# Head sums of the recurrence in two rounded passes over high and low parts

## What is computed

```python
kk = (k * k_k).reshape(B, T, 16, 64)
kk = kk / jnp.maximum(jnp.linalg.norm(kk, axis=-1, keepdims=True), 1e-12)
k = k * (1.0 + (aa - 1.0) * k_a)
# per step of the scan, for each head
sa = S @ (-kk_t)
S = S * w_t + outer(sa, kk_t * a_t) + outer(v_t, k_t)
o_t = S @ r_t
# after it
o = (o - mu) * lax.rsqrt(var + GN_EPS)      # mean and variance over a head
bonus = jnp.sum(r * k * r_k, axis=-1, keepdims=True) * v
o = (o * ln_x_w + ln_x_b + bonus) * g
```

## Time and profile before

| | |
|---|---|
| median of 3 runs | 3679.46 us |
| lowest, highest | 3678.01, 3684.09 us |
| profiled execution, its own time | 3674.07 us |
| its span | 3672.3 us |
| mean granted TensorE clock | 0.991 |
| busy: PE, PEld, DVE, ACT, POOL | 98%, 80%, 49%, 36%, 9% |

### The profile page before, as it was taken

The page is one execution under the profiler, slowest core; times in us unless marked ns, Lnnn a source line. Parts: engine busy times, 40 slices in busy tenths (PEclk is TensorE's granted clock), DMA queues, the critical chain, the costliest instruction groups (busy, mean ns, idle before and its releaser), DMA issues.

```text
span 3672.3 us, 51366 instructions
## 1 busy us (share of the span) xinstructions
PE 3617.2 (98%) x22108; PEld 2955.7 (80%) x22108; DVE 1786.2 (49%) x2455; ACT 1310.1 (36%) x2020; POOL 327.7 (9%) x328
## 2 busy tenths in 40 slices
PE   9999999999999999999999999998999999999998
PEld 8888888877788887888888888886777777688887
DVE  5435434455543455443344354344657767555444
ACT  5544222344432232332235442224342332433222
POOL 2011101100110111110110111012000000000001
PEclk9999999999999999999999999999999999899999
DMA  6212332321323233332332123323222222532322
GB/s 228 75 55 90 97 98 92 98 70 55 100 89 106 90 98 89 95 98 92 101 95 70 55 92 95 98 92 100 83 62 78 77 63 65 178 103 89 103 91 73
DMA packets 334087, 337.56 MB, mean 92 GB/s; under 512 B 12082, under 2 KB 324004, under 8 KB 333605
## 3 DMA queue, kind: packets, MB, share of 16 engines
q1 hardware_dynamic: 333572, 334.20, 29.5%
q10 hardware_dynamic: 288, 0.09, 0.0%
HBM read 319.55 MB, written 14.68 MB: 91 GB/s over the span
## 4 chain that ended last, share of the span: by engine, by line
PE 93%; DVE 4%; ACT 2%; issue 0%; ACTq 0%; POOL 0%; POOLq 0%; DVEq 0%
PE P L99 92%; PE P L102 2%; ACT sA L114 1%; DVE lo L117 1%; DVE rw_S L117 0%; DVE aL L125 0%; DVE ds L125 0%; DVE x L125 0%; DVE x L117 0%; ACTq L160 0%; POOL acc L117 0%; DVE sA L125 0%; DVE rw_k L125 0%; DVE rw_S L125 0%; ACT hi L113 0%
## 5 line engine op out<-in xcount | busy, mean ns | idle before, releaser
L99 PE MATMUL P<-aH,lo 128*128 128x512 f32 x2840 | 1132.4, 399 | 14.4 <-DVE aL L125 7.1
L99 PE MATMUL P<-aH,hi 128*128 128x512 f32 x2840 | 1109.8, 391 | 0.0
L99 PE MATMUL P<-aL,hi 128*128 128x512 f32 x2840 | 1109.5, 391 | 0.0
L113 ACT ACTIVATE hi<-raw 128x1024 fp32r<-128x1024 f32 (+2 forms) x617 | 611.5, 992 | 1026.1 <-PE P L99 1021.6
L117 DVE TENSOR_TENSOR lo<-raw,hi 128x1024 fp32r<-128x1024 f32 (+2 forms) x617 | 742.0, 1219 | 239.1 <-ACT hi L113 239.0
L99 PEld LDWEIGHTS P<-aH,lo 128*128 128x128 f32 x2840 | 534.9, 188 | 143.1 <-issue 21.4
L99 PEld LDWEIGHTS P<-aH,hi 128*128 128x128 f32 x2840 | 534.5, 188 | 112.9
L99 PEld LDWEIGHTS P<-aL,hi 128*128 128x128 f32 x2840 | 535.4, 189 | 109.4 <-issue 3.4
L99 PE MATMUL P<-bH,lo 128*128 128x512 f32 x1088 | 423.9, 390 | 0.6 <-DVE hold L117 0.6
L99 PE MATMUL P<-bL,hi 128*128 128x512 f32 x1088 | 423.7, 389 | 0.0
L99 PE MATMUL P<-bH,hi 128*128 128x512 f32 x1088 | 423.7, 389 | 0.0
(11 more groups left out here) (289 smaller groups left out, 3834.4 us busy)
## 6 DMA issues: line engine op xcount, KB each, us to landing
raw<-in_w_ffn_in_dram SPq DMA_DIRECT2D x176, 512.0 KB, 3.6
raw<-in_w_in_dram SPq DMA_DIRECT2D x163, 512.0 KB, 3.8
raw<-in_w_ffn_out_dram SPq DMA_DIRECT2D x96, 384.0 KB, 3.0
raw<-in_w_ffn_dram SPq DMA_DIRECT2D x36, 512.0 KB, 3.8
raw<-in_w_o_dram SPq DMA_DIRECT2D x26, 512.0 KB, 3.4
raw<-in_w_ffn_dram SPq DMA_DIRECT2D x32, 384.0 KB, 3.3
raw<-in_w_mem_kv_dram SPq DMA_DIRECT2D x16, 512.0 KB, 6.1
raw<-in_w_ffn_out_dram SPq DMA_DIRECT2D x16, 512.0 KB, 3.4
```

What stands on the lines that cost most here:

```text
L99: return self.e.matmul(out, l, r, start=start, stop=stop, skip_group_check=skip) if self.e else Nothing()
L113: return self.e.activation(out, in_, func, scale=scale)
```

## The change

Two of the three head sums, of the keys' squares and of the bonus, no longer use one F32 matmul. Their operand is split like the others: ScalarE copies it in rounded form (`parts[:, 0]`), VectorE writes the rest (`parts[:, 1]`), and TensorE adds two F32R matmuls with the same block of ones, which is exact in the rounded form (`bR`, written in place of `K_BONES` once at the start). The third sum, of the variance, reads the same bits of `bR` as F32 in one full matmul. The tile `parts` lies over memory that is idle at this time, so no buffer is added. Two new steps, `rw_unit_low` and `rw_bonus_low`, hold VectorE's subtractions, and the guessed costs are set anew, so `arrange` lays out the list again. No DMA is changed.

```diff
-    out += [vec("rw_lora", pe=2.6, dve=1.75, wait=1.9), vec("rw_unit", dve=0.5, gap=0.8, gives=[("kk2", p)])]
+    out += [vec("rw_lora", pe=2.6, dve=1.75, wait=1.9), vec("rw_unit", dve=0.5, gap=1.5, gives=[("kk2 high", p)])]
     out += proj("v", 2, 2)
-    out += [Step("rw_square", p, u, pe=0.9, needs=[("kk2", p)]), vec("rw_norm", dve=0.68, gap=2.6, gives=[("inverse", p)])]
+    out += [vec("rw_unit_low", dve=0.69, wait=0.0, needs=[("kk2 high", p)], gives=[("kk2", p)])]
+    out += [Step("rw_square", p, u, pe=0.5, needs=[("kk2", p)]), vec("rw_norm", dve=0.68, gap=2.6, gives=[("inverse", p)])]
...
-            vec("rw_bonus", dve=1.45, needs=[("shift", "r", p), ("key", p)], gives=[("rk", p)]), vec("rw_centre", dve=1.4),
-            vec("rw_decay", pe=0.9, dve=1.4, hold=True, needs=[("rk", p)]), vec("rw_turn", 0, pe=0.6),
+            vec("rw_bonus", dve=1.45, needs=[("shift", "r", p), ("key", p)], gives=[("rk high", p)]), vec("rw_centre", dve=1.4),
+            vec("rw_bonus_low", dve=0.69, wait=0.0, needs=[("rk high", p)], gives=[("rk", p)]),
+            vec("rw_decay", pe=0.5, dve=1.4, hold=True, needs=[("rk", p)]), vec("rw_turn", 0, pe=0.6),
...
+    def sum_heads(b, u):
+        e.mm(bank(b), m["bR"][:, :], m["rw"][u]["parts"][:, 1, :], True, False)
+        return e.mm(bank(b), m["bR"][:, :], m["rw"][u]["parts"][:, 0, :], False, True)
+
     def rw_square(p, u):
-        e.wait_ge(*S.rw_act[u].at((p, "kk2")))
+        e.wait_ge(*S.rw_act[u].at((p, "kk2 high")))
+        e.wait_ge(*S.rw_dve[u].at((p, "kk2 low")))
         take(3 * u)
-        e.mm(bank(3 * u), K.const(K_BONES), m["rw"][u]["S0"], True, True).then_inc(*S.rw_product[u].up((p, "kk2")))
+        sum_heads(3 * u, u).then_inc(*S.rw_product[u].up((p, "kk2")))
...
     def rw_decay(p, u):
-        e.wait_ge(*S.rw_dve[u].at((p, "rk")))
+        e.wait_ge(*S.rw_act[u].at((p, "rk high")))
+        e.wait_ge(*S.rw_dve[u].at((p, "rk low")))
         take(3 * u + 1)
-        e.mm(bank(3 * u + 1), K.const(K_BONES), m["rw"][u]["S2"], True, True).then_inc(*S.rw_product[u].up((p, "bonus")))
+        sum_heads(3 * u + 1, u).then_inc(*S.rw_product[u].up((p, "bonus")))
...
     def rw_var(p, u):
-        e.mm(bank(3 * u), K.const(K_BONES), m["rw"][u]["k"], True, True).then_inc(*S.rw_product[u].up((p, "var")))
+        e.mm(bank(3 * u), m["bR"][:, :].bitcast(F32), m["rw"][u]["k"], True, True).then_inc(*S.rw_product[u].up((p, "var")))
...
     def mem_norm():
         e.wait_ge(*S.const_in.at(0))
+        e.act(m["bR"][:, :], c[:, K_BONES:K_BONES + 128], ACT.Copy)
         e.act(m["cR"][:, :], c[:, K_NTRI:K_NTRI + 256], ACT.Copy).then_inc(*S.act_evict.up("signs"))
...
     def rw_unit(p, u):
-        e.act(A["S0"], A["kk"], ACT.Square).then_inc(*S.rw_act[u].up((p, "kk2")))
+        e.act(A["S0"], A["kk"], ACT.Square).then_inc(*S.rw_act[u].up())
+        e.wait_ge(*S.rw_act[u].now())
+        e.act(A["parts"][:, 0, :], A["S0"], ACT.Copy).then_inc(*S.rw_act[u].up((p, "kk2 high")))
...
     def rw_bonus(p, u):
+        e.wait_ge(*S.rw_product[u].at((p, "kk2")))
+        e.wait_ge(*S.rw_dve[u].at((p, "rk")))
+        e.act(A["parts"][:, 0, :], A["S2"], ACT.Copy).then_inc(*mine.up((p, "rk high")))
         e.wait_ge(*S.rw_dve[u].at((p, "before")))
...
+    def rw_unit_low(p, u):
+        A, mine = m["rw"][u], S.rw_dve[u]
+        e.wait_ge(*S.rw_act[u].at((p, "kk2 high")))
+        e.tt(A["parts"][:, 1, :], A["S0"], A["parts"][:, 0, :].bitcast(F32), ALU.subtract).then_inc(*mine.up((p, "kk2 low")))
+
+    def rw_bonus_low(p, u):
+        A, mine = m["rw"][u], S.rw_dve[u]
+        e.wait_ge(*S.rw_act[u].at((p, "rk high")))
+        e.tt(A["parts"][:, 1, :], A["S2"], A["parts"][:, 0, :].bitcast(F32), ALU.subtract).then_inc(*mine.up((p, "rk low")))
...
+    at("bR", [128], F32R, off=cc + 4 * K_BONES)
+    at("parts0", [2, S_], F32R, off=big + 4096)
+    at("parts1", [2, S_], F32R, off=big + 16384 + 4096)
```

More of the change, by code:

```diff
@@ L2026, in vector_program @@
                 diff_probs=diff_probs, diff_mean=diff_mean, first_end=first_end, rw_lora=rw_lora, rw_unit=rw_unit,
-                rw_norm=rw_norm, rw_key=rw_key, rw_bonus=rw_bonus, rw_centre=rw_centre, rw_decay=rw_decay, rw_scale=rw_scale, rw_gram=rw_gram, rw_first=rw_first, rw_level_a=rw_level_a, rw_level_z=rw_level_z,
+                rw_norm=rw_norm, rw_key=rw_key, rw_unit_low=rw_unit_low, rw_bonus_low=rw_bonus_low, rw_bonus=rw_bonus, rw_centre=rw_centre, rw_decay=rw_decay, rw_scale=rw_scale, rw_gram=rw_gram, rw_first=rw_first, rw_level_a=rw_level_a, rw_level_z=rw_level_z,
                 rw_level_b=rw_level_b, rw_level_c=rw_level_c, rw_solve=rw_solve, rw_step_a=rw_step_a, rw_step_b=rw_step_b,
@@ L2347, in memory_map @@
     for u in range(2):
-        rw = {n: m[f"{n}{u}"] for n in ("LG", "nat")}
+        rw = {n: m[f"{n}{u}"] for n in ("LG", "nat", "parts")}
         for n, sh in (("KR", [2, S_]), ("r", [S_]), ("k", [S_]), ("v", [S_]), ("lwd", [S_]), ("cs", [S_]), ("aa", [S_]), ("kk", [S_]),
```

## The result

The changed kernel takes 3690.06 us (median of 22 runs, 3683.63 to 3700.4), the kernel before 3679.73 (median of 22, 3675.23 to 3686.88). The ratio is 1.0028, with a 95% interval of 1.0021 to 1.0035: slower by 10.3 us. The forecast was 3673.0, faster by 6.7 us, in a range of 3666 to 3682. The profiled execution took 3691.74 us for a span of 3690.0, at a mean granted clock of 0.986 (0.991 before).

A forecast was written before the change was run, and what follows sets the result against it. TensorE's queue was taken to bound the kernel: cheaper products -6.6 us, with added ScalarE and VectorE work and lost cover at 0, sum -6.6, from the timed median 3679.46 to 3673 us; range 3666 to 3682.

The forecast's parts named there:

- The price of the pair: TensorE's head sums: two rounded matmuls cost 0.45 us against 0.86 for one full product; 16 products save 6.6 us.
- The projections hid their share: VectorE's two added subtractions in each round's projections, 1.2 us, cost nothing, since VectorE idles 16.5 of 44 us there.
- signs of being wrong: Pair above 0.5 us; TensorE waiting on subtraction or decayed key; VectorE on copy; held projections ending earlier, scan no sooner.
- the third term: VectorE's added subtractions, 1.2 us a round in the crowded stage: counted 0, or 4.8 us in all without slack.
- 1.8 us of slack, more than 1.2: Crowded stage: the first decayed key ends at 2909.44, TensorE takes it at 2911.23, so VectorE's added 1.2 us fits.
- The cover: Before the scan in the last three rounds: three held projection steps, about 2 us, missing; counted 0, other bound 6.1 us.
- the rule from the last round: Stretch before the scan: eight projection steps fewer, 5.4 us, made it 6.3 us shorter, so losing cover costs no stall.
- Part of it is given back by VectorE: Rival, chance 0.25: the crowded stage takes its 1.2 us each round after all, +4.8 us, ending at 3677.7.
- VectorE stands still behind ScalarE: Rival, chance 0.06: subtractions wait for copies stuck behind weight rounding, so TensorE waits; +12.6 us, 3692.
- The clock falls in the scan: Rival, chance 0.04: less cover halves the clock in the scan, 7.2 us a round, three rounds 21.6; +15.0, 3694.

The follow-up runs named there:

- e3: Against the kernel before: only the keys' squares summed by two narrow products, the bonus left in full form with its old steps; 0.9990, faster by 3.7 us.
- e8: Against the kernel before, old list: squares and bonus written rounded, one narrow product per sum, low parts left out, no instruction added in the rounds; 3671.83 us.
- e1: Narrow sums of both kinds, with copies and subtractions, in the unchanged list of the kernel before; 1.0012 of that kernel, slower by 4.4 us.
- e6: The changed kernel with the bonus's subtraction one step earlier, ahead of the centring of v, planner charged; 3679.7 us, 0.9999 of the kernel before.
- e12: The changed kernel, TensorE's order unchanged; on VectorE the centring of v moves behind the bonus's subtraction; 3679.36 us, 0.9996 of the kernel before.
- e5: The changed kernel, but the planner is told no VectorE time for the bonus's subtraction and the old bonus product cost; 1.0047 of the kernel before, slower by 17.3 us.

## Why the prediction was wrong

**Right.** TensorE's queue bounds the kernel, and its time there is worth its face where nothing is waited for (e3; e8 less what the banks caught). The price of the pair: 0.46 for 0.45. The 131 ns a matmul of the Trainium skill, TensorE: Matmul & The Clock Gate, section Back-to-back issue gap, did not show: the pair's 0.46 is 0.23 each. Copies 632 ns, subtractions 684 ns, no subtraction that waits for a copy, no effect of the block of ones or the variance. The projections hid their share: from the recurrence's TENSOR_SCAN to the last eviction of r, round 3 took 0.85 us less than before, where two products at 0.41 make 0.82. Of the signs of being wrong that the prediction named, the waits on the subtraction, the decayed key and ScalarE's copy stayed away; held projections that end much earlier before the scan, with the scan no sooner, came.

**The step that failed** is the third term, VectorE's 1.2 us in the crowded stage, costed at nothing because of "1.8 us of slack, more than 1.2". The slack was real, but it is that of the decayed key. The consumer that comes first in that queue is the bank of a held tile, and it had none: TensorE waited 0.29 us for it at 2908.30 already. With the list left as it was (e1) that wait grows to 1.61 us a round, so the 1.2 us are not free even there. The same term says "The listed costs also rise ... so the list will put more held work ahead of that matmul. Nothing, then". That sentence holds the loss. Moving the two bonus products behind the held tile took 1.7 us of TensorE's work from before it and turned them into a wait, 2.08 in each of three rounds (5.4 of the +6.2 us; the rest is the wait behind the last scan), though VectorE was no later.

**The cover** was mis-sized too. "About 2 us, three steps of held projection" were to be missing before the scan; in round 2 the last held eviction before the scan came 107.1 us after the first output of round 1, where it had come 120.7 us after it, 13.6 us earlier. By itself this cost little, as the rule from the last round had it: from the last eviction of r to the first scan matmul round 3 grew 1.07 us (80.26 to 81.33), less than its 2.08 us pause. Round 3 as a whole, from first output to first output, grew by 5.5 us (138.1 to 143.6): 4.0 lie ahead of the TENSOR_SCAN, where three more steps of projection now stand and the clock is 0.89, 1.3 in the scan, and the projections gave 0.85 back. The prediction did not foresee that the list would set the second chain behind the first. In e6 and e12 that costs 5.5 us of waits and eats nearly all that the narrow products save: this is why they come out at the time before and not at the forecast.

**The rivals.** "Part of it is given back by VectorE" named the right queue with too small a price and the wrong consumer (3677.7). "VectorE stands still behind ScalarE" did not occur. "The clock falls in the scan" did occur, in one round of the profile, and was priced at 7.2 us: the scan of round 4 took 25.67 us to its first output against 20.17, 5.5 us. But such falls come in runs of the kernel before too (its runs lie near 3677 us at a mean clock of 0.990 and near 3686 at 0.987), so it decides nothing alone. Over its 22 runs the changed kernel's median clock is 0.987 against 0.990. That the pauses of 2 us bring this about fits the windows above and e12 (no fall in the crowded stretch), and the Trainium skill, TensorE: Matmul & The Clock Gate, section A second HAM failure mode, speaks of short pauses between groups of matmuls that make the clock swing; here it agrees at 2771.9 and not at 2916.3, where the same pause was followed by a clock of 1.00. At 3058.9, in round 4, it agrees again. e12 is weaker support than it looks: its mean clock is still 0.988, with a fall behind the wait before the second variance product (0.60 from 2850 to 2855). In the profiled pair, 17.7 us apart, the falls can be priced: behind the two pauses eight starts each stand 0.43 and 0.41 us apart instead of 0.227, 1.6 and 1.5 us, and the last scan takes its 5.5, 8.6 us in all. How much of this the median execution holds no run shows. So the ledger's +5.6 is shown, and the 4.7 us up to the measured 10.3 are put down to the clock by argument.

## What to carry to other kernels

In a queue that runs without idle time, slack has to be read for every consumer of it, and first for the one that already waits a little: a row like [0.29 <-DVE hold] marks a place where time taken from the waiting engine ahead of it can come back as a longer wait, as the 1.7 us did here. When a planner's costs change, lay out the new order before pricing the edit, and look for what changed places; here the order alone cost 17.7 us with no work added, and one swap on VectorE gave 10.7 back. When a part is added to a crowded queue, try first which of its neighbours can go behind it, or an idle engine even if that one takes twice as long.

## What the runs showed that was not expected

A pause of 2.08 us of TensorE in a stream of 98% busy was followed in rounds 2 and 4 by some 3.4 us at the lower clock, with starts 0.43 apart instead of 0.227 (2773.11, 2773.54), and in round 3 by none; in pauses of 5.4 us the clock fell in all three rounds of e5 that had one, for 6.8 us. A fall in the scan cost 5.5 us in the changed kernel (25.67 against 20.17) and 6.3 in e3 (25.24 against 18.93), less than the 7.2 us of array time that half the clock would double by the prediction's working. Why it is less no run shows; part of each scan ran at the full clock, and in part of it TensorE waits for other engines.
